# A streaming hybrid layer on one core: one ones-matmul for each head norm, and gate logits from split operands in one pass

## The reference

```python
xn = rmsnorm(x, attn_pre_norm)
h = xn @ w_in                       # q, k, v, low-rank gate, output gate, sparse q/k/v, indexer, merge gates
log_a = log_sigmoid(g_low @ w_gla_gate_up + b_gla_gate) / 16      # g_low has 16 columns, the product 512
gla_o, gla_s = gla_recurrence(g_q, g_k, g_v, log_a, gla_s0)       # 4 heads, key width 128, value width 256
gla_o = rmsnorm(gla_o, gla_head_norm) * silu(g_r)                 # the norm is over the 256 values of one head
dsa_o = dsa_mixer(...)                                            # top-k sparse attention, 8 query heads
mixed = (gate_a * (gla_o @ w_branch_gla) + gate_b * (dsa_o @ w_branch_dsa)) @ w_out
x = x + rmsnorm(mixed, attn_post_norm)                            # then a convolutional FFN with its own norms
```

## Time and profile before

| | us |
|---|---|
| median of 3 runs | 1022.88 (1022.4 to 1023.09) |
| the profiled execution | 1022.95 |
| its span in the profile | 1021.2 |
| PE busy | 998.8 |
| DVE busy | 543.6 |
| ACT busy | 386.7 |

### The profile page before, as it was taken

One profiled execution on the slowest core, in us unless ns is written; L12 is line 12 of the kernel. 1 busy time (PEld: TensorE's weight loads), 2 busy tenths in 40 slices (PEclk: granted clock), 3 DMA queues, 4 the chain that ended last, 5 costly groups with the idle time before them and its releaser, 6 DMA issues.

```text
span 1021.2 us, 17140 instructions
## 1 busy us (share of the span) xinstructions
PE 998.8 (98%) x6814; PEld 942.8 (92%) x6814; DVE 543.6 (53%) x838; ACT 386.7 (38%) x667; POOL 86.2 (8%) x247
## 2 busy tenths in 40 slices
PE   4999999999999999999999999999999999999997
PEld 4999999888999999999997899999999999888886
DVE  5238978754322266614454768666666666312214
ACT  5343435766322246421224645333333333312212
POOL 4100000000022101002000001000000001000000
PEclk9999999999999999999999999999999999999999
DMA  7612121111232125438346433232233232312323
GB/s 244 139 57 76 49 83 42 42 42 43 89 105 65 54 99 176 141 109 269 108 152 234 134 125 89 83 84 83 83 83 85 82 88 84 107 62 83 92 103 114
DMA packets 103956, 104.25 MB, mean 102 GB/s; under 512 B 13634, under 2 KB 88242, under 8 KB 103904
## 3 DMA queue, kind: packets, MB, share of 16 engines
q1 hardware_dynamic: 97600, 81.06, 26.7%
q0 software_dynamic: 6304, 22.47, 6.3%
HBM read 89.84 MB, written 13.67 MB: 101 GB/s over the span
## 4 chain that ended last, share of the span: by engine, by line
PE 94%; ACT 2%; DVE 1%; issue 1%; DMA 1%; SPq 0%; ACTq 0%; DVEq 0%
PE ps L1388 19%; PE ps L1390 19%; PE ps L1389 19%; PE ps L1397 7%; PE ps L1399 7%; PE ps L1398 7%; PE ps L1550 2%; PE ps L1528 2%; PE ps L1407 1%; PE ps L1408 1%; PE ps L1536 1%; PE ps L1512 1%; PE ps L1476 1%; PE ps L1591 1%; PE ps L1468 1%
## 5 line engine op out<-in xcount | busy, mean ns | idle before, releaser
L1388 PE MATMUL ps<-xs,whi 128*128 128x288 f32 x1312 | 391.8, 299 | 0.2 <-issue 0.2
L1390 PE MATMUL ps<-xs,wlo 128*128 128x288 f32 x1312 | 386.6, 295 | 0.0
L1389 PE MATMUL ps<-xs,whi 128*128 128x288 f32 x1312 | 386.3, 294 | 0.0
L1388 PEld LDWEIGHTS ps<-xs,whi 128*128 128x128 f32 x1312 | 246.2, 188 | 1.7 <-issue 0.8
L1389 PEld LDWEIGHTS ps<-xs,whi 128*128 128x128 f32 x1312 | 246.2, 188 | 0.7 <-issue 0.2
L1390 PEld LDWEIGHTS ps<-xs,wlo 128*128 128x128 f32 x1312 | 246.1, 188 | 0.0
L1040 DVE TENSOR_TENSOR wlo<-raw,whi 128x2048 fp32r<-128x2048 f32 (+2 forms) x45 | 99.5, 2212 | 143.4 <-ACT whi L715 143.3
L715 ACT ACTIVATE whi<-raw 128x2048 fp32r<-128x2048 f32 (+2 forms) x47 | 86.2, 1833 | 100.4 <-PE ps L1399 88.0
L1397 PE MATMUL ps<-whi,xs 128*128 128x256 f32 (+2 forms) x264 | 86.1, 326 | 0.0
L1399 PE MATMUL ps<-wlo,xs 128*128 128x256 f32 (+2 forms) x264 | 83.3, 316 | 0.0
L1398 PE MATMUL ps<-whi,xs 128*128 128x256 f32 (+2 forms) x264 | 83.3, 316 | 0.0
(11 more groups left out here) (269 smaller groups left out, 1518.2 us busy)
## 6 DMA issues: line engine op xcount, KB each, us to landing
raw<-in_w_up SPq DMA_DIRECT2D x44, 512.0 KB, 5.0
raw<-in_w_in SPq DMA_DIRECT2D x21, 1024.0 KB, 5.6
raw<-in_w_down SPq DMA_DIRECT2D x10, 1024.0 KB, 5.1
raw<-in_w_out SPq DMA_DIRECT2D x6, 1024.0 KB, 5.1
gate_scratch<-stage POOLq DMA_DIRECT2D x16, 288.0 KB, 2.6
gates_in<-gate_scratch POOLq DMA_DIRECT2D x8, 576.0 KB, 4.3
raw<-in_w_branch_gla SPq DMA_DIRECT2D x4, 1024.0 KB, 5.1
silu_scratch<-stage POOLq DMA_DIRECT2D x8, 288.0 KB, 4.8
```

Source lines behind the costliest of these rows:

```text
L1388: pe.matmul(out, wh[:, k, c0:c0 + P], xh[:, k, t], start=(k == 0), stop=False)
L1389: pe.matmul(out, wh[:, k, c0:c0 + P], xl[:, k, t], start=False, stop=False)
L1390: ins = pe.matmul(out, wl[:, k, c0:c0 + P], xh[:, k, t], start=False, stop=(k == kn - 1))
```

## The change

- `glow` and `wgu` become of the rounded type. `glow` now holds in rows 0 to 15 and again in rows 32 to 47 the rounded low-rank gate, in rows 64 to 79 its remainder; `wgu` holds the rounded weights in rows 0 and 64, their remainder in rows 32. One product over the 128 rows then gives hi by hi, hi by lo and lo by hi together. The weights arrive in `wgu_in`, which lies where the first norm's scratch (`junk`) and later `tmp` lie; so SP waits for `xlo_ready` to reach 10 before it issues this transfer, instead of for a zero fill. ACT makes four copies into `glow` instead of two and two into `wgu`; DVE makes three subtractions.
- Head norm: after ACT's squares (`sq_made`) DVE adds the second half to the first (`sq_ready`), and PE multiplies only the sum by the ones, two matmuls instead of four.

```diff
-        glow = at("glow", [P, T], F32, o1 + 25504)
-        wgu = at("wgu", [P, GH * DK], F32, o1 + 27808)
+        glow = at("glow", [P, T], F32R, o1 + 25504)
+        wgu = at("wgu", [P, GH * DK], F32R, o1 + 27808)
...
+        wgu_in = at("wgu_in", [P, GH * DK], F32, o2 + 17408)
...
-                    sp.wait_ge(pads_zero, 1)
-                    sp.dma_start(wgu[0:RANK, :], A["w_gla_gate_up"][0]).then_inc(state_loaded, 16)
+                    sp.wait_ge(xlo_ready, 2 * TILES)
+                    sp.dma_start(wgu_in[0:RANK, :], A["w_gla_gate_up"][0]).then_inc(wgu_loaded, 16)
                     sp.dma_start(state[:, 0, :, :], A["state_gla"][0, 0].rearrange("h d v -> d h v")).then_inc(state_loaded, 16)
...
-                    nc.scalar.activation(glow[0:RANK, DEC:T], ps[0:RANK, 4, :], ACT.Copy)
-                    nc.scalar.activation(glow[0:RANK, 0:DEC], ps[0:RANK, 7, 384:448], ACT.Copy).then_inc(keys_ready, 1)
+                    for r in (slice(0, RANK), slice(32, 32 + RANK)):
+                        nc.scalar.activation(glow[r, DEC:T], ps[0:RANK, 4, :], ACT.Copy)
+                        nc.scalar.activation(glow[r, 0:DEC], ps[0:RANK, 7, 384:448], ACT.Copy)
+                    act.wait_ge(wgu_loaded, 16)
+                    nc.scalar.activation(wgu[0:RANK, :], wgu_in[0:RANK, :], ACT.Copy)
+                    nc.scalar.activation(wgu[64:64 + RANK, :], wgu_in[0:RANK, :], ACT.Copy).then_inc(gates_hi, 1)
...
-                    nc.scalar.activation(tmp[:, 0:2, :], got[:, 2 * n:2 * n + 2, :], ACT.Square).then_inc(sq_ready, 1)
+                    nc.scalar.activation(tmp[:, 0:2, :], got[:, 2 * n:2 * n + 2, :], ACT.Square).then_inc(sq_made, 1)
...
+                elif op == "keyt":
+
+                    dve.wait_ge(gates_hi, 1)
+                    nc.vector.tensor_tensor(wgu[32:32 + RANK, :], wgu_in[0:RANK, :], wgu[0:RANK, :].bitcast(F32), ALU.subtract).then_inc(gates_split, 1)
+                    nc.vector.tensor_tensor(glow[64:64 + RANK, DEC:T], ps[0:RANK, 4, :], glow[0:RANK, DEC:T].bitcast(F32), ALU.subtract)
+                    nc.vector.tensor_tensor(glow[64:64 + RANK, 0:DEC], ps[0:RANK, 7, 384:448], glow[0:RANK, 0:DEC].bitcast(F32), ALU.subtract)\
+                        .then_inc(keys_ready, 1)
...
+                elif op == "square":
+                    dve.wait_ge(sq_made, n + 1)
+                    nc.vector.tensor_tensor(tmp[:, 0, :], tmp[:, 0, :], tmp[:, 1, :], ALU.add).then_inc(sq_ready, 1)
...
+                    if slot.i == 0:
+                        pe.wait_ge(gates_split, 1)
+                        pe.wait_ge(keys_ready, 1)
...
-                        for d in range(2):
-                            ins = pe.matmul(ps[:, 4 + j, 0:HALF], ones[:, :], tmp[:, d, HALF * j:HALF * j + HALF],
-                                            start=(d == 0), stop=(d == 1))
+                        ins = pe.matmul(ps[:, 4 + j, 0:HALF], ones[:, :], tmp[:, 0, HALF * j:HALF * j + HALF], start=True, stop=True)
```

More of the change, by code:

```diff
@@ L360, in layer_kernel @@
         gpre_loaded, coefs_loaded, cache_loaded = sem("gpre_loaded"), sem("coefs_loaded"), sem("cache_loaded")
-        state_loaded = sem("state_loaded")
+        state_loaded, wgu_loaded = sem("state_loaded"), sem("wgu_loaded")
+        gates_hi, gates_split = sem("gates_hi"), sem("gates_split")
         raw_loaded = [sem("raw_loaded0"), sem("raw_loaded1")]
@@ L382, in layer_kernel @@
             sem("pads_zero"), sem("krem_ready"), sem("sc_masked"), sem("state_ready"), sem("got_copied"))
-        sq_ready, norm_summed, head_root, head_out = (
-            sem("sq_ready"), sem("norm_summed"), sem("head_root"), sem("head_out"))
+        sq_made, sq_ready, norm_summed, head_root, head_out = (
+            sem("sq_made"), sem("sq_ready"), sem("norm_summed"), sem("head_root"), sem("head_out"))
         silu_loaded, ghi_ready, glo_ready, dhi_ready, dlo_ready = (
@@ L579, in _ @@
             nc.gpsimd.memset(restart[:, :].rearrange("p (n c) -> p n c", c=CHUNK)[:, :, 0:1], 0.0).then_inc(consts_ready, 1)
-            nc.gpsimd.memset(wgu[:, :], 0.0).then_inc(pads_zero, 1)
-            nc.gpsimd.memset(glow[:, :], 0.0).then_inc(pads_zero, 1)
+            nc.gpsimd.memset(wgu[:, :].bitcast(F32), 0.0).then_inc(pads_zero, 1)
+            nc.gpsimd.memset(glow[:, :].bitcast(F32), 0.0).then_inc(pads_zero, 1)
             nc.gpsimd.memset(kz[:, :, :], 0.0).then_inc(pads_zero, 1)
@@ L1582, in aux @@
                         if tt == 0:
-                            pe.wait_ge(state_loaded, 32)
+                            pe.wait_ge(state_loaded, 16)
                         else:
```

## The result

| | before | changed |
|---|---|---|
| median, us | 1022.88 (1021.29 to 1023.52, 19 executions) | 1024.82 (1022.11 to 1025.55, 19 executions) |
| profiled execution, us | 1022.95, span 1021.2 | 1025.32, span 1023.6 |

The ratio is 1.0018, with a 95% interval of 1.0011 to 1.0024: the changed kernel is 1.9 us slower, at the edge of what can be told from no change. The forecast was 1023.1 in a range of 1021.0 to 1025.0. The range held the time. The likeliest case's own range, 1022.2 to 1024.0, did not. So the number came out, but not by the case that was called likeliest.

The account below looks back on a forecast made before the run. TensorE, busy 98% of the span, was taken as the bound, so removed matmuls pay only where it would not then wait. 1022.9 - 1.06 (gate blocks) + 1.25 (head 0) + 0 = 1023.1 us, range 1021.0 to 1025.0.

Parts of the forecast that it names:

- likeliest case: Whole kernel: gate saving and head 0's cost nearly cancel, 1023.1 us, own range 1022.2 to 1024.0, chance 0.60.
- rival B: Head 0's sum: a 3.0 us wait brings TensorE's clock to half rate, costing 1.5 to 3.0 us; 1025.2 us, chance 0.12.
- Gate blocks: Four blocks in the attention steps: of 2.84 us less TensorE work, 1.06 arrives, capped by waits for ACT's copies.
- Head 0's wait: Head 0's sum: DVE's add behind `dlo` starts PE 2.23 us later, fewer records return 0.97; net cost 1.25 us.
- Heads 1 to 3: Their sums: a 0.87 us wait for the add behind `glo` plus restart cancels the 0.97 saved; 0 per head.
- The start and the preparation: Panel 2's later landing and the splitting of `glow` and `wgu` stay covered before PE needs them; cost 0.
- Rival E: Start: panel 2 shares the engines with panel 3, is ready at 40.8, 1.5 us late; 1024.6 us, chance 0.09.
- landings at the start come in issue order: Start: the remark held against panel 2 being late, that transfers land in the order issued.
- C: Gate blocks: ACT's and DVE's attention chain follows PE, so 2.84 us arrive instead of 1.06; 1021.3 us, chance 0.15.
- D: Gate blocks and head sums: all 6.7 us arrive, adds hidden too; 1016.2 us, chance 0.04.

Follow-up runs that it names:

- gate_only: The changed kernel with the earlier head norm back (squares release TensorE directly, four ones-matmuls a head, no add), leaving only the gate part; 1021.74 us, ratio 0.9987.
- all_first: The changed kernel with all four heads' squares and adds put ahead of `dhi`/`dlo` and `ghi`/`glo` on ScalarE and VectorE; 1016.53 us, ratio 0.9942.
- before_idle: The kernel before, with an add into an unused tile behind `dlo` for which head 0's sum waits; 1025.47 us, ratio 1.0026.
- changed_again: The changed kernel measured once more, unaltered; 1024.76 us, ratio 1.0013.
- norm_only: The kernel before with only the changed head norm (add on VectorE, two ones-matmuls a head), run twice; 1024.02 and 1026.26 us, ratios 1.0019 and 1.0027.

## Why the prediction came out as it did

The range of 1021.0 to 1025.0 held 1024.82, by 0.2 us and partly by luck. The near half of rival B was in the range, and falls of 1.4 us and executions without one pulled the median down. The profiled execution, with a fall of 2.79 us, took 1025.32. The work and the waits were forecast well, and the likeliest case missed by one term.

**Gate blocks: right.** Forecast 0.45 + 0 + 0 + 0.61 = 1.06. The trace has 0.56 from the first block to the second, 0.00 over the next two, and 0.53 behind the fourth (`gate_only`): 1.09. So one cap was 0.11 too low and one 0.08 too high. Each cap stood in rows of the two engines that PE was about to wait for.

**Head 0's wait: right.** Forecast 2.23 us later, less 0.97. From the fourth gate block the sum comes 143.01 - 140.78 = 2.23 later, and PE's four records fewer give 0.97 back. (The trace counts idle from the end of the record ahead, 2.87 us. From where the next matmul could have started, 0.13 us behind the last start, it is 3.02, and at head 1 it is 0.85 instead of 0.70; 3.04 and 0.87 were forecast.)

**Heads 1 to 3: right.** Forecast 0 each. The distance between sums is 14.66 and 14.65 in both kernels. `all_first` shows what was lost there: head 0's to head 1's sum takes 14.65 with the wait and 13.69 without.

**The start and the preparation: right.** Panel 2 was forecast to land at 33.6 and be ready at 37.8, and the split gates at 58.6:

```profile
33.33 1.92 ACT L717 ACTIVATE whi<-raw 128x2048 fp32r<-128x2048 f32 x1 [7.46 <-DMA raw<-in_w_in]
...
35.28 2.29 DVE L1046 TENSOR_TENSOR wlo<-raw,whi 128x2048 fp32r<-128x2048 f32 x1 [7.80 <-ACT whi L717]
...
57.93 0.20 DVE L1103 TENSOR_TENSOR glow<-ps,glow 16x64 fp32r<-16x64 f32 x1
```

That is 37.6 and 58.1, and PE waits for neither. Rival E didn't happen: panel 2's transfer, issued at 26.98, landed at 33.31, and the next, issued 0.55 us later, at 34.54. The prediction's remark that landings at the start come in issue order holds for the weights, but not throughout: in the trace of before a cache transfer issued at 10.76 landed at 16.96, ahead of the weights issued at 9.95, which landed at 17.46. And `gate_only`, which has all of this, is faster than before. The 0.60 us that the profiled execution of the changed kernel was ahead at the first gate block comes from the stretch that answers to the earlier trace rows:

```profile
17.00:20.00 3.00, 3.00 (x15) 3.00 (x14) 2.68 (x5) 2.50 (x5) 0.00 (x0) 1.00 0.00 0
20.00:23.00 3.00, 3.00 (x24) 2.97 (x23) 2.57 (x3) 1.09 (x2) 0.00 (x0) 1.00 0.00 0
```

**Rivals C and D.** C falls with the waits of 1.57 and 1.40 us. D, 1016.2, "needs DVE's adds ahead of `dlo` and `glo`": in that order the kernel took 1016.53. It had been worked out as a ceiling only; it was also the recipe.

## What to carry to other kernels

When work moves from a busy engine to an idle one, find its place in the idle engine's queue first: the add of 0.75 us delayed PE by 2.2 us where a subtraction that nobody needed soon stood in front of it, by 0.8 us ahead of that subtraction, and not at all where the squares too stood ahead. Moving the squares and the add forward for all heads turned 1.9 us of loss into 6.5 us of gain. On TensorE price a new idle of the lengths that brought a fall here (2.3 us and more at head 0, once 1.73 us elsewhere) twice, once as idle and once as the half rate that may follow it, and read the clock column and the instruction count behind it, since the busy share shows neither. A median can lie between two clusters; look at the single executions and their clock before explaining it.

## What the hardware showed that was not expected

- The same program with the same idle of 2.87 us kept the clock in some executions and lost it in others: 10 of 22 fell with the head norm part alone, 27 of 31 with the gate part beside it, 7 of 8 with 3.5 us. What decides was not found. Counted from the first gate block, the idle begins 1.1 us later in the first of these (210.24 against 209.18), and the executions stood on different chips; no run separates either.
- A fall at head 0 had one of two sizes, read as what it added between head 0's and head 1's sum: about 1.4 us (1.36 in `before_idle`, 1.44 in `changed_again`) or about 2.8 (2.79 in the first profile of the changed kernel and in `norm_only`, 2.73 in its second). The clock was low for 3.4 us in the short ones and for 6.8 in the long ones.
- One execution fell a second time, at 478 us, behind a wait of 1.73 us that a late transfer had made.
- In the first profile of the changed kernel PE was busy from 371.51 to the end of the low stretch at 377.56, so the busy share hid it; ones-matmuls of 288 columns ran at about twice their length (0.85 us for the longest record, 0.41 for the usual one), projections 0.24 apart instead of 0.13.
- Twenty matmuls without a use, inside a wait that exists anyway, saved 2.1 us.
